# Half-size block products by Strassen's scheme in the input projection, and transposed blocks moved by DMA, in a one-core differential-attention layer

## The reference

```python
def diff_attention(u, w_in, w_out, ...):
    proj = u @ w_in                       # 512 x 2048 by 2048 x 8192
    q, k = 16 heads of 128;  v = 8 heads of 256;  z = 2048 columns
    # per pair of heads: causal softmax of q k^T * scale + bias, for both
    a = p[:, :, 0] - lam * p[:, :, 1]
    o = rms_norm(a @ v, subln_g) * (1.0 - lam_init)
    return (o * silu(z)) @ w_out          # 512 x 2048 by 2048 x 2048
h = layer_norm(alpha * x + diff_attention(x, ...), ln_g, ln_b)
```

## Time and profile before

| | |
|---|---|
| median of 3 runs | 942.35 us (942.32 to 942.46) |
| the profiled execution | 942.39 us |
| its span, first to last instruction | 940.6 us |
| PE busy | 934.3 us, 99%, 4202 matmuls |
| PE weight load busy | 777.6 us, 83% |
| DVE busy | 550.5 us, 59% |
| ACT busy | 318.1 us, 34% |
| POOL busy | 66.4 us, 7% |
| granted TensorE clock | 1.000 of 2.4 GHz |

### The profile page before, as it was taken

The page is one execution under the profiler, slowest core; times in us unless marked ns, Lnnn a source line. Parts: engine busy times, 40 slices in busy tenths (PEclk is TensorE's granted clock), DMA queues, the critical chain, the costliest instruction groups (busy, mean ns, idle before and its releaser), DMA issues.

```text
span 940.6 us, 11611 instructions
## 1 busy us (share of the span) xinstructions
PE 934.3 (99%) x4202; PEld 777.6 (83%) x4202; DVE 550.5 (59%) x1131; ACT 318.1 (34%) x558; POOL 66.4 (7%) x140
## 2 busy tenths in 40 slices
PE   9999999999999999999999999999999999999997
PEld 8888888888888888888888888888888888888886
DVE  5546764766466646664666466646664797324466
ACT  4423333333333333333333333333333454122311
POOL 2200010001000100010001000100000000000033
PEclk9999999999999999999999999999999999999999
DMA  8732342223222322232224222422232223542423
GB/s 317 270 104 72 100 132 97 82 95 134 93 85 94 135 92 86 94 135 91 87 92 137 90 88 89 139 89 89 90 112 89 89 90 122 201 159 90 157 103 121
DMA packets 34087, 108.88 MB, mean 116 GB/s; under 512 B 4352, under 2 KB 6400, under 8 KB 33808
## 3 DMA queue, kind: packets, MB, share of 16 engines
q1 hardware_dynamic: 28320, 93.60, 29.5%
q0 software_dynamic: 2336, 9.48, 3.0%
q10 hardware_dynamic: 3408, 5.51, 1.7%
HBM read 104.34 MB, written 9.48 MB: 121 GB/s over the span
## 4 chain that ended last, share of the span: by engine, by line
PE 99%; DMA 0%; DVE 0%; issue 0%; ACT 0%; SPq 0%; DVEq 0%; ACTq 0%
PE proj L1003 79%; PE att L1003 20%; DMA w_raw<-w_in_tiles_dram 0%; DVE big L995 0%; DVE last_stats L981 0%; ACT bias L654 0%; SPq L322 0%; DVE w_split L851 0%; DVE mean_var L984 0%; DVEq L983 0%; ACTq L653 0%
## 5 line engine op out<-in xcount | busy, mean ns | idle before, releaser
L1003 PE MATMUL proj<-w_split,xg_split 128*128 128x512 f32 x1680 | 385.2, 389 | 0.0
L1003 PEld LDWEIGHTS proj<-w_split,xg_split 128*128 128x128 f32 x1680 | 314.8, 188 | 65.2
L1003 PE MATMUL proj<-xg_split,w_split 128*128 128x512 f32 x1536 | 353.0, 389 | 0.2 <-DVE w_split L851 0.2
L1003 PEld LDWEIGHTS proj<-xg_split,w_split 128*128 128x128 f32 x1536 | 287.5, 188 | 59.6 <-issue 0.5
L460 ACT ACTIVATE w_split<-w_raw 128x1024 fp32r<-128x1024 f32 x128 | 135.8, 1061 | 383.6 <-PE proj L1003 354.5
L675 DVE TENSOR_TENSOR w_split<-w_raw,w_split 128x1024 fp32r<-128x1024 f32 x128 | 155.5, 1224 | 175.6 <-ACT w_split L460 173.8
L749 DVE STREAM_TRANSPOSE scratch<-scratch 32x192 f32<-32x192 f32 (+2 forms) x384 | 141.8, 369 | 5.2
L1003 PE MATMUL att<-w_split,xg_split 128*128 128x512 f32 x432 | 99.9, 389 | 0.0
L1003 PEld LDWEIGHTS att<-w_split,xg_split 128*128 128x128 f32 x432 | 81.0, 188 | 16.8
L928 DVE TENSOR_TENSOR w_split<-w_raw,w_split 128x1024 fp32r<-128x1024 f32 x25 | 30.5, 1225 | 58.1 <-ACT w_split L619 58.0
L421 POOL TENSOR_SCALAR mean_sq<-sq_sum 128x1 f32<-128x1 f32 x32 | 10.3, 323 | 701.6 <-ACT scratch L511 700.3
(11 more groups left out here) (116 smaller groups left out, 428.1 us busy)
## 6 DMA issues: line engine op xcount, KB each, us to landing
w_raw<-w_in_tiles_dram SPq DMA_DIRECT2D x126, 512.0 KB, 3.3
w_raw<-w_out_tiles_dram SPq DMA_DIRECT2D x32, 512.0 KB, 3.3
bias_by_distance<-bias_lines POOLq DMA_DIRECT2D x8, 640.0 KB, 5.1
bias<-bias_by_distance POOLq DMA_DIRECT2D x8, 512.0 KB, 4.1
x_res<-in_x_dram ACTq DMA_DIRECT2D x4, 1024.0 KB, 6.2
big<-x_cols_dram SPq DMA_DIRECT2D x7, 512.0 KB, 9.1
out_dram<-big SPq DMA_DIRECT2D x10, 256.0 KB, 2.5
w_raw<-w_in_tiles_dram SPq DMA_DIRECT2D x4, 256.0 KB, 4.7
```

Source lines behind the costliest of these rows:

```text
L1003: return nc.tensor.matmul(dst, lhsT, rhs, start=start, stop=stop, skip_group_check=True)
```

## The change

For pairs 1 to 7 the first eight of the sixteen k-tiles are computed by Strassen's scheme (in Winograd's form). The left factor is cut into four blocks (4 k-tiles by 256 rows of x), the weights of q with k, and of v with z, into four blocks (4 k-tiles by 256 columns). Seven block products take the place of eight. A block product is 24 matmuls with 256 moving columns. A pair is now two phases (q and k; v and z) of 11 slots: seven products, then four slots as before for k-tiles 8 to 15.

What the scheme adds:

- four sums of blocks of x, made once in pair 0 (`x_sum`, `x_sum_hi`, `x_sum_lo`), which lie over the raw x;
- four sums of weight blocks in each phase on DVE (`w_sum`), each 128 x 1024, and the hi/lo split of the summed tiles like any other tile, so 22 splits per pair where there were 16;
- partial results that enter more than one block of the output: ACT copies regions out of PSUM (`keep_copies`, `keep_corners`), DVE adds them (`keep_sums`) and seeds other regions with the sums (`seed_corners`, `seed_highs`), and PE waits for these before products 4, 5 and 6 of a phase.

The transposes of pairs 0 to 6 change as well. DVE does one instruction over all 128 partitions, which transposes every 32 x 32 block in place, and POOL then moves the blocks between partition groups with 16 SBUF-to-SBUF DMAs (`swap_blocks`). This is done once for a (DVE at the end of slot 21, read by ACT in slot 5 of the next pair) and once for the gated result (DVE in slot 10, read by ACT in slot 15). g is stored to DRAM pair by pair and loaded again before the output projection, since its place in SBUF now holds the sums of x. The last pair keeps the old transposes. `weigh_v` moves to after slots 6 and 8, the scores to after slots 16 and 18, and `g_early` of the last pair to after slot 21.

The diff, cut to its core:

```diff
+NB = P // B
+SK = 4
+HALF_SEQ = SEQ // 2
+PHASE = 11
+SLOTS = 2 * PHASE
...
+            def swap_blocks(dst, src_at, done):
+                n = dst.shape[2]
+                for i in range(NB):
+                    for j in range(NB):
+                        pool.dma_start(dst[j * B:(j + 1) * B, i],
+                                       scratch[i * B:(i + 1) * B, src_at + j * n:src_at + (j + 1) * n]
+                                       ).then_inc(done, 16)
...
+                if p + 1 < PAIRS:
+                    load_bias(p + 1)
+                    pool.wait_ge(a_turned, p + 1)
+                    swap_blocks(aT_blocks, 0, aT_done)
...
+            def seed_corners(p, h):
+                for group in range(2):
+                    n = 2 * (phases_before(p) + h) + group + 1
+                    dve.wait_ge(copy_kept, 3 * (phases_before(p) + h) + group + 2)
+                    low, corner = region(h, group, 1, 0), region(h, group, 1, 1)
+                    nc.vector.tensor_tensor(low, low, kept_sum[:, group], ALU.add).then_inc(low_seeded, 1)
+                    dve.wait_ge(low_seeded, n)
+                    nc.vector.tensor_tensor(corner, low, kept_copy[:, group], ALU.add).then_inc(corner_seeded, 1)
...
+            def turn_a(p):
+                dve.wait_ge(a_ready, p * ST + ST)
+                nc.vector.transpose(a_blocks, a_rows.rearrange("p n (b c) -> p n b c", b=NB)).then_inc(a_turned, 1)
...
+            def slot(p, j):                      # DVE
+                h, r = j // PHASE, j % PHASE
+                if j == PHASE:
+                    k_chunk(p)
+                if 17 <= j < 20:
+                    logits_of(p, j - 17)
+                if j == 20:
+                    combine(p, 2)
+                    logits_of(p, 3)
+                split_lo_at(p, j)
+                if r == 0:
+                    w_sum(p, h, 4)
+                if r == 2:
+                    keep_sums(p, h)
+                if r == 3:
+                    seed_corners(p, h)
+                if r == 4:
+                    seed_highs(p, h)
+                late_steps(p - 1, j)
...
+                if j == 21:
+                    combine(p, 3)
+                    if not last_pair(p):
+                        turn_a(p)
+                if j == 20 and last_pair(p):
+                    turn_last_a(False)
...
+            def product(p, j):
+                h, r = j // PHASE, j % PHASE
+                pe.wait_ge(w_ready, slots_before(p) + j + 1)
...
+                opens = r in (0, 2)
+                for group in range(2):
+                    if opens and h == 0:
+                        bank = 2 * group + side
+                        pe.wait_ge(vz_moved, p * ST - ST + bank + 1)
+                        pe.wait_ge(max_ready, p * (2 * ST) - (2 if bank < 2 else 0))
...
+                    elif r == 4:
+                        pe.wait_ge(sum_kept, phases_before(p) + h + 1)
+                    elif r == 5:
+                        pe.wait_ge(corner_seeded, 2 * (phases_before(p) + h) + group + 1)
+                    elif r == 6:
+                        pe.wait_ge(high_seeded, 2 * (phases_before(p) + h) + group + 1)
...
+            def inserts(p, j):
+                if j == 6:
+                    weigh_v(p - 1, (0, 1))
+                if j == 8:
+                    weigh_v(p - 1, (2, 3))
+                if j in (16, 18):
+                    scores_of(p, j - 16)
+                    scores_of(p, j - 15)
```

More of the change, by code:

```diff
@@ new lines, in in_fours, with out_raw, out_raw_count, phase_banks @@
+        def in_fours(flat):
+            return flat.rearrange("p (k n) -> p k n", k=SK)
+        def out_raw(n):
+            return OUT_RAW[(n - TOTAL) % RING]
+        def out_raw_count(n):
+            i = out_raw(n)
+            return 16 * (EARLIER[i] + PER_PAIR[i] * (PAIRS - 1) - (1 if i < RING else 0) + (n - TOTAL) // RING + 1)
+        def phase_banks(h, side):
+            banks = proj[:].rearrange("p b (c n) -> p b c n", c=2)
+            return banks[:, side::2] if h == 0 else banks[:, 2 * side:2 * side + 2]
@@ L283, in x_unit_of, with split_a, gated_of, wait_a_turned @@
+        def split_a(t, part):
+            return aT[:, t % 2, part, 0:(t + 1) * P].rearrange("p (n b c) -> p n b c", b=NB, c=B)
+        def gated_of(p, t):
+            return (last_gated if last_pair(p) else gated)[:, t]
+        def wait_a_turned(eng, p, t):
+            if last_pair(p):
+                eng.wait_ge(last_aT_done, 1 if t < ST - 1 else 2)
+            else:
+                eng.wait_ge(aT_done, SWAP * (p + 1))
         def x_unit_of(k):
@@ L458, in split_hi_at @@
-                if not (first_pair(p) and j == 0):
-                    act.wait_ge(quarter_done, p * QUARTERS + j)
-                nc.scalar.activation(split_view(a, 0), w_raw[:, ring(a)], ACT.Copy).then_inc(w_hi, 1)
+                if first_pair(p):
+                    if a < QUARTERS:
+                        split_first(a)
+                    else:
+                        split_in(1, a - QUARTERS)
+                elif a < SLOTS:
+                    split_in(p, a)
+                elif last_pair(p):
+                    split_out(TOTAL + a - SLOTS)
+                else:
+                    split_in(p + 1, a - SLOTS)
@@ new lines, in last_g_copy @@
+            def last_g_copy():
+                act.wait_ge(last_nT_done, 1)
+                for e in range(2):
+                    dst = g[:, 2 * (PAIRS - 1) + e]
+                    nc.scalar.activation(dst.rearrange("p (t s) -> p t s", t=ST), last_gT[:, :, e], ACT.Copy,
+                                         scale=sub_g[:, e:e + 1]).then_inc(g_ready, 1)
+            def late_steps(p, j):
+                if j == 5:
+                    aT_split(p, 0)
+                    aT_split(p, 1)
+                tiles = {7: (0, 1), 9: (2, 3)}.get(j, ())
+                for t in tiles:
+                    copy_low(p, t)
+                if j == 7:
+                    aT_split(p, 2)
+                    aT_split(p, 3)
+                for t in tiles:
+                    norm(p, t)
+                if j == 15:
+                    g_copy(p)
@@ L739, in combine @@
                 dve.wait_ge(mix_ready, n)
+                if t == 0 and not first_pair(p):
+                    dve.wait_ge(g_stored, 16 * p)
                 cols = slice(0, (t + 1) * P)
@@ L871, in _ @@
             for j in range(QUARTERS):
-                slot(0, j, False)
+                first_slot(j)
+                if j in X_SUMS_AT:
+                    for i in X_SUMS_AT[j]:
+                        x_sum(i)
                 if j in (1, 3, 5):
```

651 lines of the change are left out of this document (479 added, 172 removed).

## The result

The changed kernel takes **930.72 us** (median of 4, 929.69 to 931.81) where the kernel before took 942.4: ratio 0.9874, 95% interval 0.9857 to 0.9891. The forecast was 923.6 with a range of 914 to 937, so faster, as forecast, but with 11.7 us of the expected 18.8. The profiled execution took 931.81 us, with a span of 929.6; by it 8.2 us are to be found.

What follows compares the result with a forecast made beforehand. PE's own pace was taken to bound the kernel, for 99% of the span. From 942.4 us, products gain 25.8, boundary waits add 3.3 and the last pair 3.7: 923.6 us, range 914 to 937.

Steps and rivals of the forecast that it cites:

- band of 919 to 929: Whole kernel: the main forecast, products gaining and waits added at pair ends, given a chance of 0.57.
- late seeds and boundaries: Rival, more waits than walked: seeds late by 1 us per phase or boundaries by 1.5, 937 us; chance 0.17.
- The products: PE's stream: 168 matmuls of 256 columns a phase at 0.1186 us; 1.84 us gained per phase, 25.8 over 14.
- the bound of 0.130: Upper end for a 256-column matmul, from the scores' ten in 1.17 us; at it the change loses 1 us.
- The fourth rival, slow weights: Long product runs: weight loads too slow, 0.135 us a matmul, kernel at 962 us; chance 0.04.
- Waits inside a phase: Splits and seeds before products: no wait, 1.4 to 2.4 us to spare; other end 1 us per phase, 14 us.
- The end of a pair: PE waits 0.55 us for the first bank at six boundaries, 3.3 us; ends 0 and 30 us.
- The pair of 90.9 us among the signs: Sign that the prediction is right: a pair takes 90.9 us in the new kernel.
- The last pair: After pair 7, before the output projection: PE waits 3.7 us once for the first bank; ends 2 and 5.
- The blocks by DMA: POOL's 16 block DMAs: 12 + 5 = 17 us, hidden within 19.3 us, costing nothing.
- the third rival: At `weigh_v` after product 6: block DMAs land late, PE waits, kernel slower, 969 us at 1.3 us an issue; chance 0.07.
- Around the span: Time of the profiled execution outside its span: 1.8 us, within the starting 942.4 us.

## Why the prediction was right, and where it was short

The sign, the range and the main mechanism held: PE bounds the kernel, and the products shorten its stream. But 923.6 was 8.2 us short of the profiled execution, and the time lies outside the band of 919 to 929 that had 0.57. The range reached to 937 for late seeds and boundaries, and no seed was late; half of the 8.2 us are two costs that the prediction did not have, a slow clock behind a wait and POOL's drain. That the range held is in part luck. Term by term:

- **The products.** 25.8 us were forecast from 0.1186 us a matmul. It is 0.120 in 2352 of them, so a phase gains 1.60 us, not 1.84, and the change 22.4: **3.4 us of the 8.2**. The value was read from seven matmuls of `weigh_v`, where an edge of 10 ns is worth 1.4 ns a matmul. The six of the earlier trace rows and the bound of 0.130 enclosed it. The fourth rival, slow weights, did not come (72 in a row hold 0.120, not 0.135), but it was near: with the weight load at 0.112, 256 columns are just above it, and fewer columns would have gained almost nothing.
- **Waits inside a phase.** Nothing was forecast and nothing came. With slots of 1.44 us the same sums and seeds are waited for, so the room was real and finite.
- **The end of a pair.** 0.55 us at each of six were forecast. The idle gap is 0.35, but a pair with it takes 91.62 us (278.82 to 370.44) and one without 91.01, so a boundary costs 0.61, 3.7 us in all against 3.3: **0.4 us**. With the turn behind the banks 3.6 us came back. The transpose of 1280 elements took 1.51 us, by forecast 1.5. (The pair of 90.9 us among the signs does not follow from the prediction's own terms: 94.22 - 2 x 1.84 + 0.55 = 91.1.)
- **The last pair.** 3.7 us forecast; 3.71 from 736.40 to 740.11. Missing was what an idle PE pays next: 7.15 us for 5.44, **1.7 us**, shown by the filled wait and by the removed one.
- **The blocks by DMA.** Hidden, as forecast, with 10.5 us in place of 17. Doubled, they make PE wait where the third rival says. Their hidden price is at the end: POOL's drain, 6.4 us in place of 2.5, of which **2.4 us** are past all else. The early drain took them off, so they are work left over by DMAs of POOL. What the length goes by stays open, but the record has half of a rule: less the 1.09 us that are left after an early drain, it is 0.084, 0.083 and 0.081 us a DMA for 17 and 31 of them (512 and 640 KB but for one) and 129 (most of 40 KB). By this estimate 241 and 465 both leave only as much as 65 would; whether the rest is done earlier there, and where, is not shown.
- Around the span: 2.2 us, not 1.8, **0.4 us**.

The sum again with what was measured: 942.4 - 22.4 + 3.7 + 3.7 + 1.7 + 2.4 + 0.4 = 931.9, against 931.81.

## What to carry to other kernels

Price a wait of PE with the clock behind it: here 3.5 us idle cost up to 2.8 more, and the cure was to move work of DVE into gaps that it had two slots earlier. Where the engine that made PE wait is late for the next slot too, the slow clock hardly costs anything. Before cutting matmuls in two, compare the new column time with the weight load: at 256 columns there was 7% left. Look at each queue's drain at the end of the program when a queue gets a new kind of work; one drain in an idle stretch took 7.2 us off where the last one was 11.6 us long.

## What the runs showed of the hardware

- A matmul of 256 columns with weights of 128 costs 0.120 us in a long run, of 128 columns 0.112, and of 128 columns with weights of 64 columns 0.060 (the last two in one execution each).
- A wait of 3.2 to 3.6 us was followed by granted clocks of 0.53 (over 2.2 us), 0.65 (8.24 us) and 0.76 (7.2 us); at 0.53 the engine is near its lower level, 1.2 GHz, and these windows hold both levels. A wait of 2.33 us was followed by 0.62 (4.47 us) in one pair and by 1.00 (586.10 to 590.18) in another. Behind six gaps of 0.35 us the window of the pair stood at 1.00.
- A DMA that POOL issues between partitions took 0.50 us to issue, at 40 KB, 32 KB and half of these, next to 0.70 to 0.80 for those to and from DRAM, and landed after 2.5 to 3.0 us by the median. DVE's additions run beside the sets (L918 at 188.97 and L981 at 190.10 beside the one of 186.71), and the mean of 448 is still 500 ns: no run here shows an issue lengthened by DVE.
- A transpose over 128 partitions (1.25 us for 1024 elements, 1.51 for 1280) lies on the line of those over 32 (0.44 us for 256, 0.52 for 320): 0.17 us and 1.05 ns an element, with no price for the other partitions.
- POOL's drain at the end took 1.1 us after an early drain, and else 2.5, 3.7, 11.6, 6.4 and 6.4 us with 17, 31, 129, 241 and 465 DMAs of POOL in the program; the waits view put a wait for it down to PE's queue.
